# Feed-forward by nested seven-product multiplication: outer products started half a product apart, results added straight from the banks, sums of the normed activations stored once and loaded in later rounds

## What is computed

```python
def finish(x, y_gla, y_nsa, w_out, norm_mix_post, norm_ffn_pre, norm_ffn_post, w_ff_up, w_ff_down):
    y = jnp.concatenate([y_gla, y_nsa], axis=-1) @ w_out
    x = x + rms_norm(y, norm_mix_post)
    h = rms_norm(x, norm_ffn_pre)
    u = jnp.square(jax.nn.relu(h @ w_ff_up))          # 1024 -> 4096
    return x + rms_norm(u @ w_ff_down, norm_ffn_post)  # 4096 -> 1024
```

## Time and profile before

| | us |
|---|---|
| median of 3 runs (1918.2 to 1925.33) | 1921.0 |
| profiled execution, its own time | 1916.28 |
| its span, first to last instruction | 1914.4 |
| feed-forward loop, first inner product to the end of the last | 1128.58 to 1894.77 |
| what follows the loop (last norm, stores) | 19.6 |

### The profile page before, as it was taken

One profiled execution on the slowest core, in us unless ns is written; L12 is line 12 of the kernel. 1 busy time (PEld: TensorE's weight loads), 2 busy tenths in 40 slices (PEclk: granted clock), 3 DMA queues, 4 the chain that ended last, 5 costly groups with the idle time before them and its releaser, 6 DMA issues.

```text
span 1914.4 us, 25746 instructions
## 1 busy us (share of the span) xinstructions
PE 1759.3 (92%) x9958; PEld 1413.0 (74%) x9958; DVE 1155.4 (60%) x1902; ACT 616.6 (32%) x1282; POOL 806.9 (42%) x539
## 2 busy tenths in 40 slices
PE   7999999978999799999979987999999998999897
PEld 6888888855555477776758876888778877877786
DVE  5232211557766565556430287897689868976897
ACT  3311211368877744444410341120111012101212
POOL 3222121334444421222201378656574658455842
PEclk9999999979999999999979988999999999999999
DMA  5011232050000395767451230121001110111004
GB/s 141 23 45 50 69 70 66 2 184 29 7 7 10 124 339 210 276 210 257 140 187 45 98 134 1 44 66 67 34 13 64 67 45 22 45 67 44 1 1 177
DMA packets 89344, 166.48 MB, mean 87 GB/s; under 512 B 21616, under 2 KB 55064, under 8 KB 80968
## 3 DMA queue, kind: packets, MB, share of 16 engines
q1 hardware_dynamic: 80008, 97.73, 15.8%
q0 software_dynamic: 9216, 67.11, 9.6%
HBM read 148.35 MB, written 20.66 MB: 88 GB/s over the span
## 4 chain that ended last, share of the span: by engine, by line
PE 57%; DVE 12%; issue 7%; ACT 1%; POOL 1%; DMA 1%; DVEq 0%; ACTq 0%
PE PS L2908 27%; PE PS L1990 8%; PE PS L305 5%; DVE srow L2957 4%; PE PS L1794 4%; PE PS L1779 4%; PE PS L1807 3%; DVE Z L2998 2%; DVE Z L2957 1%; PE PS L2000 1%; PE PS L479 1%; PE PS L2123 1%; PE PS L2008 1%; POOL Z L1638 1%; PE PS L2160 1%
## 5 line engine op out<-in xcount | busy, mean ns | idle before, releaser
L2998 DVE TENSOR_TENSOR Z<-PS,Z 128x516 f32<-128x516 f32 x292 | 197.0, 688 | 113.4 <-PE PS L2908 113.2
L2925 ACT ACTIVATE Z<-PS 128x516 f32<-128x516 f32 x100 | 60.0, 600 | 510.1 <-PE PS L2908 510.1
L2908 PE MATMUL PS<-srow,misc 128*128 128x258 f32 x560 | 137.9, 394 | 26.5 <-DVE srow L2957 16.3
L2908 PEld LDWEIGHTS PS<-srow,misc 128*128 128x128 f32 x560 | 108.2, 195 | 47.5 <-issue 18.9
L2908 PE MATMUL PS<-Z,X 128*128 128x258 f32 x600 | 140.3, 381 | 0.2 <-DVE Z L2998 0.2
L2957 DVE TENSOR_TENSOR Z<-Z 128x2064 f32<-128x2064 f32 x49 | 125.3, 2563 | 19.3 <-ACT Z L2925 18.5
L1990 PE MATMUL PS<-Z 128*128 128x256 f32 x512 | 129.0, 389 | 0.0
L2908 PEld LDWEIGHTS PS<-Z,X 128*128 128x128 f32 x600 | 113.9, 190 | 17.1 <-DVE Z L2998 0.6
L2908 PE MATMUL PS<-srow,X 128*128 128x258 f32 x496 | 121.2, 389 | 4.0 <-DVE srow L2957 2.2
L1517 POOL DMA_INDIRECT Z<-in_cache_nsa_kv,idx x48 | 49.2, 1026 | 167.8 <-ACT X L2194 97.8
L1100 DVE TENSOR_TENSOR Z<-PS,Z 128x516 f32<-128x516 f32 x27 | 18.8, 696 | 166.7 <-PE PS L305 166.7
(11 more groups left out here) (456 smaller groups left out, 4100.2 us busy)
## 6 DMA issues: line engine op xcount, KB each, us to landing
X<-in_w_ff_down SPq DMA_DIRECT2D x12, 1024.0 KB, 7.1
ring<-in_w_in SPq DMA_DIRECT2D x9, 1024.0 KB, 5.1
X<-in_x_prompt SPq DMA_DIRECT2D x8, 1024.0 KB, 8.6
ring<-in_w_ff_up SPq DMA_DIRECT2D x8, 1024.0 KB, 5.5
Z<-in_w_ff_up SPq DMA_DIRECT2D x8, 1024.0 KB, 7.5
out_y_prompt<-X SPq DMA_DIRECT2D x16, 512.0 KB
Z<-in_w_ff_down SPq DMA_DIRECT2D x4, 1024.0 KB, 4.9
X<-out_y_prompt SPq DMA_DIRECT2D x4, 1024.0 KB, 5.1
```

The source lines that it names most:

```text
L2908: last = nc.tensor.matmul(M.PS[:, N_.bank(n, e) + c, 0:HB], x[:, k, c * P:(c + 1) * P], y[:, k, :], start=e in (M1, M2, M5) and k == 0, st ...
L2925: nc.scalar.activation(N_.inner_out(n, e), N_.view(n, e), ACT.Copy).then_inc(N_.act, 1)
L2998: nc.vector.tensor_tensor(x, N_.view(n, e), x, ALU.add).then_inc(N_.dve, 1)
```

## The change

1. **Half a product apart.** Outer product n+1 starts when n has done half its inner products: inner product e of n stands in slot 7n + 2e, so that neighbours interleave for half their length each, in place of both starting together. The bank rule (the move of the product four places before) stays. The order of the outer products within a round changes too (`data`, `weights`, `READY_W`).
2. **Results added from the banks.** The places of U11, U12, U22, A1X1 to A7X2 go. Where a result is wanted twice (outer products 4, 7, 9, 11 of a round, `TWICE`), VectorE takes each inner result from the bank twice; for the others it adds it to what is there already, or to a neighbour's place. ScalarE copies only the four first results of outer product 0 of a round; it also zeroes the output places once, in round 0.
3. **Sums kept in memory.** In round 0 the sums t2 to t4 of outer products 0 to 6 (21 of 264 KB) and T2H, T3H, T4H (3 of 1 MB) are stored to two new DRAM tensors. In rounds 1 to 3 SyncE loads them back in place of VectorE's work (`move_sum`, `move_outer`).
4. Small things: GpSimd's first weight sums no longer wait for the activations; the first inner product waits for its weights alone; PSUM banks and residual loads of the last norm are ordered for the new end; some semaphores of an earlier phase are given back after it.

```diff
+    TWICE = (4, 7, 9, 11)
     @staticmethod
     def slot(n, e):
-        return 14 * (n // 2) + 2 * e + n % 2
+        return 7 * n + 2 * e
...
-    def by_act(self, n, e):
-        return self.fresh(n) and e in (M1, M6, M5, M4)
+    def reloaded(n):
+        return n >= RNG and n % RNG < 7
+    def by_act(n, e):
+        return n % RNG == 0 and e in (M1, M6, M5, M4)
...
+    def move_sum(self, sp, n, i):
+        g, j = divmod(n, RNG)
+        buffer, kept = self.t(n, i), self.kept_sums[3 * j + i]
+        if g == 0:
+            self.wait_t(sp, n, i)
+            sp.dma_start(kept, buffer).then_inc(self.sum_dma[i][j % 2], 16)
+            return
+        self.wait_product(sp, n - 2, (M6, M7, M4)[i])
+        if i == 0 and not self.reloaded(n - 2):
+            self.wait_t(sp, n - 2, 2)
+        sp.dma_start(buffer, kept).then_inc(self.sum_dma[i][j % 2], 16)
+
+    def move_outer(self, sp, g, what):
+        n = RNG * g
...
+        self.wait_chain(sp, n + {"T2H": -4, "T3H": -1, "T4H": 2}[what])
+        if what == "T2H":
+            self.wait_d(sp, g - 1, "T4U")
+        sp.dma_start(buffer, kept).then_inc(self.outer_dma[what], 16)
...
+            if j == 7:
+                moved(y(0, 0), n, e, y(0, 0))
+                moved(y(1, 1), n, e, y(1, 1))
+            if j == 8:
+                moved(y(0, 1), n, e, y(0, 1))
+            if j == 9:
+                moved(y(1, 1), n, e, y(1, 1))
+                moved(y(1, 0), n, e, y(1, 0), ALU.subtract)
...
             if e == M1:
-                N_.wait_w(pe, g, READY_W[j])
+                if n == 0:
+                    N_.wait_loaded(pe, g, 0)
+                else:
+                    N_.wait_w(pe, g, N_.READY_W[j])
```

More of the change, by code:

```diff
@@ L2912, in _ @@
         pe.wait_ge(hwr, 2 * (QT + 1))
[L2913 to L2919 removed]
+        for s in range(SLOTS):
+            if at_slot(s) is None:
+                continue
+            n, e = at_slot(s)
+            if n == NC - 1 and e in (M7, M3):
+                norm.turn(pe, e - M7)
+            product(n, e)
     @block_.scalar
     def _(act):
[L2923 to L2925 removed]
         def square(g, k, t, i):
@@ new lines, in _ @@
+        dve.wait_ge(hwr, 2 * (QT + 1))
+        prepare(0, 0)
+        for s in range(SLOTS):
+            if s == 0:
+                data_sum(0, 0)
+                prepare(1, 0)
+            if s == 1:
+                prepare(0, 1)
+            if s == 2:
+                dve.wait_ge(N_.prep, 3)
+                nc.vector.tensor_tensor(N_.h(0, 1), N_.h(0, 1), N_.h(0, 0), ALU.subtract).then_inc(N_.prep, 1)
+            if s == 3:
+                prepare(1, 1)
+            if s // 98 < ROUNDS:
+                outer(s // 98, s % 98)
+            for i, ahead in enumerate((-3, 1, 5)):
+                n = (s - ahead) // 7
+                if (s - ahead) % 7 == 0 and n < NC and not N_.reloaded(n):
+                    data_sum(n, i)
+            if s == 7 * (NC - 3) + 14:
+                N_.wait_out(dve, NC - 3)
+                nc.vector.tensor_tensor(N_.y(1, 0), N_.y(1, 0), N_.y(1, 1), ALU.add).then_inc(N_.last, 1)
+            if s == 7 * (NC - 3) + 16:
+                nc.vector.tensor_tensor(N_.y(0, 1), N_.y(0, 1), N_.y(1, 1), ALU.add).then_inc(N_.last, 1)
+            if at_slot(s) is None:
+                continue
+            n, e = at_slot(s)
+            if n == NC - 1 and e in (M3, M4):
+                norm.scale(dve, e - M3)
+            if not N_.by_act(n, e):
+                move(n, e)
@@ L3139, with build @@
 ]
-def build(nc, A, O):
+def build(nc, A, O, K):
     M = Mem()
+    M.kept_sums, M.kept_outer = K["sums"], K["outer"]
     with ExitStack() as ctx:
```

568 lines of the change are left out of this document (302 added, 266 removed), and 17 rows, old and new, of tables (DVE_STEPS, POOL_STEPS).

## The result

The changed kernel takes 1873.99 us in the median of four runs (1869.57 to 1877.51), the kernel before 1923.0 beside it (1918.2 to 1925.33): a ratio of 0.9747, with a 95% interval from 0.9713 to 0.9782. Forecast were 1869 us. The profiled execution of the changed kernel took 1870.59 us, its span 1868.9, its feed-forward loop ran from 1128.52 to 1846.55.

What follows compares the result with a forecast made beforehand. TensorE, busy 92%, loses 82.2 us in the loop, mostly to VectorE held up by GpSimd. Losses fall to 33: gain 49 + 1.9 = 51, 1916.3 to 1865; median put at 1869 us, own range 1857 to 1887.

Steps and rivals of the forecast that it cites:

- Slots 0 to 45 of rounds 1 to 3 without a stop: Feed-forward loop: only moves and one transform against 80 us, no stop; gives back 8.7 and most of 6.2 us.
- the tolerance of 4.3 us: How late a VectorE move may be before TensorE, needing its bank four slots on, stops: 4.3 us.
- Slots 46 to 75: Rounds 1 to 3, VectorE's work packed here: collisions with GpSimd sum to 4.9, taken as 5 us a round, bounds 0 and 12.
- The doubled moves: VectorE's moves rise from 74 to 122 a round, 30 to 33 us more, none on the path by themselves.
- Round 0: First round, forming and storing everything: 10 us lost up to slot 30, 5 in the second half; together 15.
- I cost them at nothing: Added loads and stores in SyncE's queue: no cost, no weight block held by more than a few slots.
- Start: First product of the loop: GpSimd does its transforms in earlier idle time, gain 1.9 us.
- End: Last three products run without a neighbour: 1 us more in the loop, nothing after it; bounds -2 and +2.
- the case without a stop: Rival: GpSimd's steps fall between the sums, rounds 1 to 3 lose nothing; gain 76, 1845 us (1840 to 1857); chance 0.15.
- The dearer half: Rival: packed slots 46 to 75 cost more, losses 72, gain 12; 1909 us, case 1887 to 1911; chance 0.20.
- The slower one: Rival: stored-sum loads come late in SyncE's strict order; gain gone at landings of about 27 us, 1945 at 30; chance 0.05.
- the cover: Time a sum's buffer is free before TensorE wants its new content: 14 slots, 24 us, for a load to land.

Runs made afterwards that it cites:

- e4_no_kept: The changed kernel without the stored sums, all sums formed in every round, stagger and adds from the banks kept: 1871.0 us, ratio 0.9741.
- b1_before_quarters: The kernel before, with GpSimd's sums of whole places each issued as four instructions of 512 columns: 1854.2 us, ratio 0.9662.
- b4_s1_early: The kernel before, with GpSimd forming the whole place S1 and its two transforms ahead of the first weight sums: 1900.4 us, ratio 0.9891.
- e2_a21: The changed kernel, with SyncE in round 0 issuing the loads of A21 and A12 ahead of two stores of sums: 1871.0 us, ratio 0.9746.
- e3_quarters: The changed kernel, with GpSimd's sums of whole places each issued as four instructions of 512 columns: 1862.7 us, ratio 0.9705.
- b3_no_normed_sums: The kernel before, with the sums that the change stores cut to one column in rounds 1 to 3, waits kept: 1896.5 us, ratio 0.9869.
- e6_bursts: e4_no_kept with the data sums of outer products 1, 3 and 5 formed right behind their neighbours' in rounds 1 to 3: 1872.1 us, ratio 0.9737.
- both of the best kernels: The changed kernel with 512-column pieces and earlier residual load: without stored sums 1849.6 us; with them and A21 ahead of two stores 1850.9 us.

## Why the prediction was right, point by point

**The total.** Forecast 1869 with 1857 to 1887 as its own range, measured 1874. Against the profiled execution the sum said 1865, it took 1870.6. The difference is made of terms that partly cancel: +7.1 in round 0, -5.4 in the others, +1.9 at the start, +2.5 at the end; the rest is rounding. That the total came so close is luck in part: round 0 was too cheap by about as much as the other rounds were too dear, and the largest term, slots 0 to 45 of rounds 1 to 3, came true for another reason than the one given.

**Slots 0 to 45 of rounds 1 to 3 without a stop.** The number was right (0), the reason was not. The step that failed is the sentence that gives back 8.7 and most of 6.2 us because "moves and one transform" stand there. e4_no_kept has all the sums there and loses nothing; b1_before_quarters gets all of it in the old order without storing a sum, and b4_s1_early 3.6 of its 10.8 us (6.4 of 13.6 in round 3) by GpSimd's order alone. What brought this term in the changed kernel is the rest of the change, through the places at which GpSimd's long sums now stand; slot 5 is owed to GpSimd's order, and for the other stops the stagger and the adds from the banks are not told apart. I had read the collisions and the tolerance of 4.3 us off the same rows, but counted meetings one by one and never asked which of them come in pairs.

**Slots 46 to 75.** Forecast 5 a round, measured 3.7. The layout was right in kind: all of TensorE's waits there are moves of VectorE, behind sums that met a whole place. By steps: DS2 met nothing, being over (at 1396.2) before the sum of slot 46 began; DS4 met the transform as said, but VectorE came to it in time, and the stop of 1.0 didn't come; T1U, forecast with 2.3, brought none; T2U cost 0.85 (0.5 forecast), and DS3 2.57 where I had 1.1. A meeting that I had not listed, of a data sum with S1 at slot 89 of rounds 0 to 2 (4.40 us), passed without a stop. The doubled moves, "none on the path by themselves", cost 2.3 of the 3.7.

**Round 0.** The first part has the right sum (10 forecast, 10.9) and other parts: I had the first move 3.4 us late and 6 more up to slot 30, but slot 4 alone lost 7.1, slots 6 and 7 another 2.9 at half clock, and slots 8 to 45 nothing. The second half was put at 5 like the others and cost 11.3. The failed step is "I cost them at nothing": "none of the weight blocks queued behind is held by more" than a few slots. That holds in rounds 1 to 3; in round 0 the stores wait for sums not yet formed, and A21 stands behind them. e2_a21 gives 5.4 of these 6.3 us back, and e4_no_kept, which stores nothing, loses 5.2 in this half.

**Start.** The gain of 1.9 us from GpSimd's earlier transforms is there: TensorE's first product no longer waits for GpSimd, as it did by 3.26 us, and begins 0.05 us after the last activations are written. But those came later in this execution, in a part of the program that the change doesn't touch. The windows ahead of the loop, of after and of before (the last three figures: clock, DMA share, GB/s):

```profile
0.00:130.00 130.00, 118.12 (x587) 99.06 (x588) 52.58 (x80) 38.68 (x61) 32.84 (x47) 0.97 0.26 75
```

```profile
0.00:130.00 130.00, 118.98 (x596) 100.17 (x597) 52.56 (x80) 40.28 (x63) 32.83 (x47) 0.99 0.27 77
```

The difference in the granted clock, 0.97 in place of 0.99, is one stretch more at the lower level (1.2 in place of 2.4 GHz): from 58.7 to 62.1 us the clock was 0.50 after and 1.00 before. That costs about half of the 3.4 us, most of the 2.0 by which the same matmul near 110 us begins later. Over the executions here the loop began between 1127.4 and 1135.9 us, both ends in kernels with the mixer and the start of the kernel before, so a gain of 1.9 there can't be read from one execution.

**End.** "Nothing after the loop" was wrong by 2.5 us. M3 of the last outer product, which releases the residual block, stands one product from the end in the new order; I had followed the moves to the norm and not the DMA. The 1 us more in the loop's last slots was 0.

**Clock.** The losses that the prediction counted include stretches at half clock behind a stop. In the kernel before, behind the stop of slot 17 in round 1:

```profile
1361.00:1364.20 3.20, 1.33 (x6) 1.22 (x7) 3.20 (x2) 0.69 (x1) 2.77 (x2) 0.99 0.00 0
1364.20:1367.60 3.40, 3.40 (x9) 2.45 (x9) 3.21 (x6) 0.60 (x1) 0.00 (x0) 0.50 0.02 5
```

By the granted clocks of the rounds (0.96, 0.99, 0.99 for round 2 as for 1, and 0.97 before; 0.96 and then 1.00 after) some 35 us of the loop ran at the lower level before, and 15 after. Half of the difference, an estimate of 10 us, is part of the 48 that the loop gained: where a stretch at half clock followed a stop that is gone, it is gone too.

**Rivals.** (The prediction's "third rival", beside the rule on the ports, is its second, the case without a stop.) The dearer half came true in round 0 alone, the case without a stop only for slots 46 to 60 of the others. The slower one, loads that come late, had its place in SyncE's queue right and its victim wrong: not a data sum in rounds 1 to 3 but a weight block in round 0. Its price was added up wrongly: landings of 30 us, 6 over the cover, would cost 21 x 6 = 126 us and give 1869 + 126 = 1995, not 1945; no load came near that.

## What to carry to other kernels

Where VectorE and GpSimd both work from SBUF, look first at the longest instruction of each and at what it holds up on the other; cutting GpSimd's 2048-column sums into four was worth 66 us here, in four lines, more than the whole change. A queue that tolerates one delay and not two in a row loses nothing or much by the same instructions, so ask of each collision what stands right behind it, and don't carry the gain of an edit over to another order of the queues. Shortening the instruction that waits doesn't help; shortening the one that is waited for does. When experiments cut an instruction short, ask whether it still waits. When the order of the products changes, go through every wait that names a product or a slot, DMAs included, and in the first round apart from the others.

## What the runs showed of the hardware that I had not expected

- Four instructions of 512 columns take GpSimd hardly longer than one of 2048 when VectorE leaves it alone: single ones took 1.27 us each, and four in a row 4.95 (e3_quarters, 1381.45), against 4.53 to 4.55. I had expected a larger price for starting three more.
- When both engines have short sums they take turns: four pieces took 7.80 us and the three sums of VectorE beside them 6.0. With long ones whoever is in front keeps the other for the whole length, GpSimd too: its sum at 1344.70 took 6.61 us in b4_s1_early beside a 2064-column sum of VectorE.
- A sum of VectorE on one column pays the whole wait: 4.48 us for two elements a row behind S4 in b3_no_normed_sums, where such sums take 0.15 us alone.
- The clock falls behind some stops and not behind others of the same length: in the kernel before behind the stop at slot 17 (3.5 us) in each of rounds 1 to 3, behind the one at slot 5 (3.45 us) only in round 3. The stop of 2.6 us at slot 63 was followed by half clock in rounds 1 to 3 of e6_bursts, and in none of them in the changed kernel. What decides it is left open; it makes some 1.7 us a time, and so is part of the differences between executions of one kernel.
- Open as well: 7.8 us in the first slots of round 0 and 1.5 to 1.7 at slot 68 of each round, which both of the best kernels still lose.
